# One table of token rows for both layers, and its blanking moved from the in-projection to the gate units

## The reference

```
hx = modulate(rms_norm(x, g_norm1), sh1, sc1);  zx = hx @ w_in          # 1024 x 5120
merged = g_a*(o_attn @ p_attn) + g_h*(o_hy @ p_hyena) + g_c*(o_cf @ p_conv)
x = x + gt1 * (merged @ w_out)                                           # attention, Hyena, Conformer
hx2 = modulate(rms_norm(x, g_norm2), sh2, sc2)
x = x + gt2 * moe(hx2, ...)    # sigmoid router, best group of 4, top 2 of its experts, 16 experts
```

## Time and profile before

| | |
|---|---|
| Median of 3 runs | 1411.58 us (1408.71 to 1411.61) |
| The profiled execution | its span is 1404.0 us; its own time outside the profiler is not recorded, the median of the runs is 7.6 us above its span |
| Busy: PE, DVE, ACT, POOL | 89%, 45%, 26%, 9% of the span |
| Mean granted TensorE clock | 0.945 |
| Chain of waits, largest shares | issue 22%, PE 21%, DMA 11%, DVE 7% |
| Bytes moved | 382.71 MB, mean 273 GB/s |
| Blanks of x_rows, of y_rows | 32 and 20 of 512 KB, median 11.0 and 12.1 us from issue to landing |

### The profile page before, as it was taken

One profiled execution on the slowest core, in us unless ns is written; L12 is line 12 of the kernel. 1 busy time (PEld: TensorE's weight loads), 2 busy tenths in 40 slices (PEclk: granted clock), 3 DMA queues, 4 the chain that ended last, 5 costly groups with the idle time before them and its releaser, 6 DMA issues.

```text
span 1404.0 us, 20024 instructions
## 1 busy us (share of the span) xinstructions
PE 1247.6 (89%) x8172; PEld 793.1 (56%) x8172; DVE 626.9 (45%) x1126; ACT 366.2 (26%) x595; POOL 124.9 (9%) x119
## 2 busy tenths in 40 slices
PE   3699898899999988999999966987999986999986
PEld 1477576787877733334343325776789852444443
DVE  2628358776547362122131116485885761221222
ACT  2622124433144310000100115433544620000000
POOL 0000000000004020000000011003960201000000
PEclk9799998999999989999999996999999998999998
DMA  9747994242213389899899983775345489999997
GB/s 380 271 186 321 398 387 185 90 91 86 94 61 122 152 326 387 290 354 347 329 356 389 415 338 149 279 321 210 117 111 176 168 343 387 388 383 397 404 415 301
DMA packets 59887, 382.71 MB, mean 273 GB/s; under 512 B 8913, under 2 KB 11413, under 8 KB 20309
## 3 DMA queue, kind: packets, MB, share of 16 engines
q1 hardware_dynamic: 45584, 345.00, 63.2%
q10 hardware_dynamic: 9748, 18.74, 4.1%
q0 software_dynamic: 4464, 17.71, 3.6%
HBM read 363.84 MB, written 44.84 MB: 291 GB/s over the span
## 4 chain that ended last, share of the span: by engine, by line
issue 22%; PE 21%; DMA 11%; DVE 7%; ACT 2%; POOL 2%; SPq 0%; DVEq 0%; POOLq 0%; ACTq 0%
DMA wexp<-in_expert 7%; PE bank L2421 3%; DMA x_rows<-trow,rowid 3%; PE bank L2015 3%; PE bank L2436 3%; PE bank L2017 3%; PE bank L2016 3%; PE bank L1982 2%; PE bank L2454 1%; DVE wlo L1255 1%; POOL x_rows L770 1%; POOL m_lo L754 1%; DMA stage<-in_in 1%; PE bank L2294 1%; PE bank L2107 1%
## 5 line engine op out<-in xcount | busy, mean ns | idle before, releaser
L2421 PE MATMUL bank<-wexp,xg 128*64 128x512 f32 (+1 forms) x1488 | 263.3, 595 | 5.0 <-DMA wexp<-in_expert 1.9
L2015 PE MATMUL bank<-h_hi,whi 128*128 128x512 f32 (+1 forms) x640 | 228.6, 357 | 21.5 <-DVE wlo L1255 13.3
L2016 PE MATMUL bank<-h_lo,whi 128*128 128x512 f32 (+1 forms) x640 | 222.8, 348 | 0.0
L2017 PE MATMUL bank<-h_hi,wlo 128*128 128x512 f32 (+1 forms) x640 | 222.6, 348 | 0.0
L2421 PEld LDWEIGHTS bank<-wexp,xg 128*64 128x64 f32 (+1 forms) x1488 | 77.8, 125 | 155.6 <-issue 145.0
L1255 DVE TENSOR_TENSOR wlo<-stage,whi 128x2048 fp32r<-128x2048 f32 x56 | 134.3, 2405 | 69.8 <-ACT whi L797 68.2
L2436 PE MATMUL bank<-wexp,act_a 128*32 128x256 f32 (+1 forms) x1072 | 145.1, 488 | 16.3 <-DMA wexp<-in_expert 12.2
L2015 PEld LDWEIGHTS bank<-h_hi,whi 128*128 128x128 f32 x640 | 127.2, 199 | 46.2 <-DVE wlo L1255 18.3
L1255 DVE TENSOR_TENSOR act_a<-act_s,bank 128x256 f32<-128x256 f32 (+1 forms) x47 | 17.1, 365 | 263.9 <-ACT act_s L797 263.9
L2016 PEld LDWEIGHTS bank<-h_lo,whi 128*128 128x128 f32 x640 | 127.0, 199 | 13.8 <-issue 0.5
L2017 PEld LDWEIGHTS bank<-h_hi,wlo 128*128 128x128 f32 x640 | 126.4, 197 | 14.0
(11 more groups left out here) (342 smaller groups left out, 1603.4 us busy)
## 6 DMA issues: line engine op xcount, KB each, us to landing
wexp<-in_expert SPq DMA_DIRECT2D x190, 1024.0 KB, 14.6
stage<-in_in SPq DMA_DIRECT2D x40, 1024.0 KB, 8.6
raw<-in_mod SPq DMA_DIRECT2D x18, 1024.0 KB, 7.9
stage<-in_mod SPq DMA_DIRECT2D x16, 1024.0 KB, 4.9
x_rows<-in_c_zero SPq DMA_DIRECT2D x32, 512.0 KB, 11.0
y_rows<-in_c_zero SPq DMA_DIRECT2D x20, 512.0 KB, 12.1
spare<-in_mod SPq DMA_DIRECT2D x8, 1024.0 KB, 14.4
stage<-in_out SPq DMA_DIRECT2D x8, 1024.0 KB, 4.8
```

The costliest lines, as they stand in the source:

```text
L2015: MM(o, w[0], x_[0], start=start, stop=False)
L2016: MM(o, w[0], x_[1], start=False, stop=False)
L2017: return MM(o, w[1], x_[0], start=False, stop=stop)
L2421: ins = MM(bank[0][g * w:(g + 1) * w, :], x_[:, 2 * j + k, :], weights[:, c], start=(first_ == 0), stop=(last_ == 0))
```

## The change

One table x_rows of 2560 rows serves both layers. The list BLANK holds its 20 blocks and the 9 blocks of y_rows from row 1408 on (the planned rows end at 1440). They are issued two at a time behind the loads of units 34 to 48 (`BLANK_AT` is 34), and POOL waits for 29 blocks.

```diff
-        x_rows = [nc.dram_tensor(f"x_rows{l}", (ROWS[l], D), f32, kind="Internal").ap() for l in range(DEPTH)]
+        x_rows = nc.dram_tensor("x_rows", (max(ROWS), D), f32, kind="Internal").ap()
+
+        BLANK = [x_rows[b * P:(b + 1) * P, :] for b in range(max(ROWS) // P)]
+        BLANK += [y_rows[b * P:(b + 1) * P, :] for b in range(plans[0].extra_base // P, ROWS[0] // P)]
...
+                BLANK_AT = order.first_gate + 2
+                assert 2 * (order.count - BLANK_AT) >= len(BLANK)
...
-                    if l == 0 and at["in", 4] <= n < at["in", 4] + ROWS[0] // P:
-                        b = n - at["in", 4]
-                        for rows_ in (*x_rows, y_rows):
-                            if b * P < rows_.shape[0]:
-                                load("all", "rows_zeroed", rows_[b * P:(b + 1) * P, :], A["c_zero"])
+                    if l == 0 and n >= BLANK_AT:
+
+                        for rows_ in BLANK[2 * (n - BLANK_AT):2 * (n - BLANK_AT) + 2]:
+                            load("all", "rows_zeroed", rows_, A["c_zero"])
...
-                    pool.wait_ge(sem("all", "rows_zeroed"), (sum(ROWS) // P + ROWS[0] // P) * 16)
+                    pool.wait_ge(sem("all", "rows_zeroed"), len(BLANK) * 16)
```

More of the change, by code:

```diff
@@ L770, in _ @@
                         pool.indirect_dma_start(
-                            out=x_rows[l], out_offset=bass.IndirectOffsetOnAxis(ap=rowid[:, 2 * t + c:2 * t + c + 1], axis=0),
+                            out=x_rows, out_offset=bass.IndirectOffsetOnAxis(ap=rowid[:, 2 * t + c:2 * t + c + 1], axis=0),
                             in_=trow[:, t, :], in_offset=None,
@@ L777, in _ @@
                     row, w = plans[l].steps[PICKED[l] + i][3:]
-                    load("all", f"yg{i}", xpick[0:w, i, :], x_rows[l][row:row + w, :])
+                    load("all", f"yg{i}", xpick[0:w, i, :], x_rows[row:row + w, :])
                 if l < DEPTH - 1:
@@ L1106, in load_rows @@
                     r = s - PICKED[l]
-                    act.dma_start(xpick[0:w, r % XR, :], x_rows[l][row:row + w, :]).then_inc(S(f"xload{r % XR}"), 16)
+                    act.dma_start(xpick[0:w, r % XR, :], x_rows[row:row + w, :]).then_inc(S(f"xload{r % XR}"), 16)
                 def silu(s, w):
@@ L1199, in _ @@
                     act.wait_ge(S("xT_mm"), s + 1)
-                    act.dma_start(xpick[0:E, LAST % XR, :], x_rows[l][bass.ds(i * E + plan.extra_base + E, E), :]).then_inc(S(f"xload{LAST % XR}"), 16)
+                    act.dma_start(xpick[0:E, LAST % XR, :], x_rows[bass.ds(i * E + plan.extra_base + E, E), :]).then_inc(S(f"xload{LAST % XR}"), 16)
                     act.wait_ge(S("act_a"), s)
```

## The result

The changed kernel takes 1390.68 us (median of 6 runs, 1389.65 to 1398.91) against 1409.09 us of the kernel before (1405.96 to 1411.61). The ratio is 0.9889, with a 95% interval of 0.986 to 0.9917; two more series gave 0.9879 (0.9852 to 0.9905) and 0.9864 (0.984 to 0.9889). These ratios are taken from all runs and are not the quotients of the medians (0.9869 for the first series). It is faster by 1.1 to 1.4%, some 16 to 19 us.

The account below looks back on a forecast made before the run. TensorE, 89% busy, bounds the kernel; transfers pay only where it stands for them, in the in-projection where DMA is full. 3.1 + 3.5 + 8.5 + 0.4 = 15.5 us, from 1411.58 to 1396.1 us; range 1391 to 1405.

Parts of the forecast that it names:

- Stall (a): In-projection near 150 us: PE stands 5.29 us for the late load of mod unit 25; forecast gain 3.1 us.
- Stall (b): First gate unit, 200.77 us: PE stands 1.90 us for wlo; with its slow block, forecast gain 3.5 us.
- Stall (c): First head, 219.83 us: PE stands 5.90 us for the softmax, through the late gate load; forecast gain 8.5 us.
- The 17 blanks at units 40 to 48: Blanks added in the gate units, claimed covered: cost taken as 0, bounds 0 and 22 us.
- One table at nothing, with 3 us either way: Scatters into the shared x table, at a new place in HBM: cost taken as 0, 3 us kept either way.
- Nothing given back after 226 us: After 226 us PE, DVE and ACT events start everything, so the lead is carried to the end.
- What lies around the span: 7.6 us between the profiled span of 1404.0 and the median 1411.58, left as they are.
- A sign that was ill chosen: At the first gate load: ACT still waiting over 10 us for it would show the forecast wrong.
- The other signs: Right if PE waits about 2 us near 150, under 1 us for probs, and first-head clock is 1.0, among others.
- the late softmax: Rival at the first head: softmax stays late by DVE's own work, 6.6 us gained, 1405.0 us; chance 0.12.

Follow-up runs that it names:

- e7: Kernel before with one x table for both layers, the second table's 12 blanks sent to a table nobody reads; 1409.46 us, ratio 1.0000.
- e1: Changed kernel with its one table and 29 blanks, but these left in the in-projection behind units 20 to 34; 1400.12 us, ratio 0.9923.
- e2: Kernel before with its three tables and all 52 blanks, moved to units 34 to 51, three behind each; 1393.58 us, ratio 0.9881.
- e4: Kernel before with the 24 blanks of units 20 to 26 and 29 moved to units 40 to 47; 1405.26 us, ratio 0.9963.
- e6: Changed kernel with four more blanks behind each of units 34 to 48, 89 in all; 1392.55 us, ratio 0.9863.
- e3: Kernel before with the 16 blanks of units 27, 28 and 30 to 33 moved to units 40 to 47; 1399.08 us, ratio 0.9906.

## Why the prediction was right

The forecast was 1396.1 us in a range of 1391 to 1405, for a gain of 15.5 us. Measured medians are 1390.7 to 1393.5, ratios 0.9864 to 0.9889, which are 15.6 to 19.2 us of 1409 to 1411. The forecast time started from 1411.58, the median of three runs; six runs gave 1409.09, so 2.5 us of the distance between 1396.1 and 1390.7 are the starting point. Mechanism and order of events are as forecast; the forecast gain is at the low end, and the first median lies 0.3 us under the range's low end while the two others lie inside. The gain is there in full at the first scatter: against the profile before it comes 14.9 us earlier in the first profile, 17.3 and 17.6 in the two others. Against e7 it is 10.9 to 13.6. The profile before has the longest D, and e7's profile is of the fastest of its ten runs (1402.98), so the typical gain in place lies between the two.

- *Stall (a), 3.1 us, or 4.7 if the clock holds.* The transposes started at 151.10 and not at the forecast 151.85 (PE is already 0.8 us earlier at unit 21, ahead of the stalls). What is late next was named rightly, DVE's product, 2.27 us against 2.0. The slow clock behind it came in the first profile and not in the two others. I took the dip as given, and that was the rare case: of the seven profiles with this stall of 2.27 us (the changed kernel's three, e1, e2, e4, e6) only the first had it. The larger value, 4.7, was the better one, and accounts for most of what the two quicker profiles gain over 15.5. The prediction's 0.6 us for the transposes at full clock is 0.8 by its own rows (1.93 less 1.09).
- *Stall (b), 3.5 us.* Gone in all three profiles. The load was issued at 173.9 and landed at 182.55; I had 174.9 and 183.8. 3.15 MB in 9.9 us from the first issue agree with 10.2. In 174:182, where no blank runs, the DMA engines moved 398 to 426 GB/s in the three profiles, so loads alone are at least as fast as the 388 that the sum used. The 1.6 us of slow block counted here were real in the profile before, but e4 and e7 had none behind stalls of 1.8 and 1.2 us. For a typical execution the sum thus has 1.6 us too little in (a) and, as far as three profiles show, up to 1.6 too much in (b); that the two offset each other is luck.
- *Stall (c), 8.5 us.* Gone. The GLU began at 186.76 (188.0 forecast), the probs ended at 205.91 (207.2), PE came at 206.16 (207.3). DVE's part was 19.15 us in both. Against e3 it is shown that (c) hangs on the gate load and not on DVE's amount of work.
- *The 17 blanks at units 40 to 48 at nothing.* Shown by e2 and e6: these 17 and 60 more behind units 34 to 48 are free.
- *One table at nothing, with 3 us either way.* Shown by e7. Layer 0's scatters landed in 27.31 us (28.71 in the earlier trace rows).
- *Nothing given back after 226 us.* The lead of 16.3 us at 209 is 16.05 at POOL's first m_lo (410.28 against 426.33) and 14.9 at the scatter, in the first profile. Between the last two stands a stretch of slow clock behind PE's wait for POOL (0.88 in 418:432; 1.00 there in another profile of the same kernel); the two other profiles kept 17.3 and 17.6.
- *What lies around the span.* I put 7.6 us, the median less the profile's span. That was wrong: the executions for which both are known have 1.8 to 3.4 us, so the profiled execution before took about 1406 us and was one of the quick ones. Its D, though, is the longest of all, so the quickness came later, in the DMA-bound stage. The forecast time rests on a gain, not on this, and the error was in its place only.
- *A sign that was ill chosen.* I named as wrong an ACT that still waits over 10 us for the first gate load. It does, 17.2 us, with no harm: it had nothing else to do. What counts is when the wait ends. The other signs came as forecast: a DMA share of 0.49 in 122:200 (about 0.5 forecast) and of 0.42 in 290:370 (about 0.4).

Of the rivals, the late softmax (1405.0) had the wrong reason, DVE's own work: e3 has no wait for probs. Its event, a softmax that stays late, happened in e1 (load at 189.08, 1400.1 us) and e4 (191.04, 1405.3 us), through the gate load. It was not far off: 6 us of landing time.

## What to carry to other kernels

Look at what a cheap transfer stands in front of, in its queue, and at how long before its use the next load is issued. Here 40 of 52 copies of zeros made PE stand 13 us where the two loads that count are issued 10 and 17 us before PE asks for them (138.30 and 148.76; 181.75 and 198.87), and 89 cost nothing in the gate units, where a load goes out 32 us ahead (unit 34: 192.5, used at 224.5). And follow a stall that names a compute engine back through its order of work: half of the forecast gain stood under "softmax late", with a transfer at the head of DVE's order, behind the split of the weights.

## What the hardware showed that I had not expected

A stall of PE of about 2 us (1.90 before, 2.27 after) is sometimes followed by some 3 us at 1.2 GHz and mostly not, in one and the same kernel. Three such stalls can be counted over the twelve profiles: that near 150 (2.27 us) was followed by it in 1 of 7, that at the first gate unit (1.8 to 1.9 us) in 1 of 2, PE's wait for POOL near 424 (2.1 to 2.2 us) in 1 of 11. Behind the stalls of 5 us and more PE ran at 1.2 GHz each time. So the cost of one short stall is its length, plus 0 or about 1.6 us (1.1 at the wait for POOL), and two executions of one kernel may differ by 3 us in the mixer of layer 0 alone. To tell changes of this size apart, more than one profile is needed.

SP needs 0.51 to 0.60 us to issue a copy of 512 KB from HBM to HBM in the windows read here. A load of 1 MB takes it 0.33 to 0.38 us where no blank goes out right before it, and 0.52 to 0.58 us right behind one (in the earlier trace rows units 25 and 32, against 24 and 30). So blanks take SP's time twice, with their own issue and with that of the load behind them.
